# A two-layer diffusion trunk on one core: 16384 experts per layer, gathered per token before, evaluated densely after

## The chip, the cores and the metric

The kernel runs on one core of one Trainium2 chip. The metric is the device time of one execution in microseconds, the median of several runs. All arrays are float32 before and after the change.

## What is computed

The trunk has two layers over 512 latent tokens and 256 context tokens of width 1024. Each layer is a mixer (a projection, four mLSTM heads, eight attention heads, an output projection, a norm) and then the PEER sub-layer, the only part that the change touches. In layer 0 it works on all 768 tokens (six tiles of 128), in layer 1 on the 512 latent ones (four tiles).

```python
q = (ub @ wq).reshape(tb, 8, 2, 128)
s1 = einsum('thd,hnd->thn', q[:, :, 0], sub_keys[:, 0])   # 128 keys per half
s2 = einsum('thd,hnd->thn', q[:, :, 1], sub_keys[:, 1])
t1, i1 = top_k(s1, 16);  t2, i2 = top_k(s2, 16)
top, pos = top_k(t1[..., :, None] + t2[..., None, :], 16)  # of 256 candidates
eidx = the 16 expert numbers i1 * 128 + i2 of each of 8 heads
g = softmax(top)
act = gelu(einsum('td,tkd->tk', ub, up[eidx]))             # 128 experts per token
y = einsum('tk,tkd->td', g * act, down[eidx])
```

`up` and `down` have 16384 rows of 1024 per layer. A token uses 128 of them (8 heads by 16). The kernel keeps both in one array, `updown`, with rows of 2048 numbers (8 KB): up first, then down.

## The kernel before

Five engines run their own programs and meet at barriers (`meet`) between stages. Conditioning rows come first, then for each layer projection, mLSTM and attention, the output projection with the first norm (L676 to L698 on TensorE, which also folds the query weights and the sub-keys into `wk`), and then the expert stage. The norm after the experts closes the layer.

The expert stage goes tile by tile, head by head, slot by slot: 128 slots per tile. A slot is one expert per token. POOL gathers 128 rows of 8 KB for it by an indirect DMA (L976) into one of eight ring buffers. DVE multiplies the up half by the modulated token and sums it (L1312). ACT takes the gelu (L920). DVE builds a diagonal matrix of gelu times gate (L1305, `make_diag`). TensorE multiplies that diagonal by the down half in two matmuls of 512 columns, which add into two PSUM banks (L723, `weigh`). Meanwhile the routing of the head after next is cut into steps that DVE runs between the slots (`route`, L1232): the scores come from TensorE (L715, eight matmuls of 256 columns per head). There are 1280 slots in the two layers. A slot's buffer comes free when its matmuls are done (`L.slot_done`), and only then is its next gather issued.

The order around the change is set by semaphores alone: TensorE's order is the program's, SP issues the loads of each stage in a fixed list, and POOL has nothing to do but the gathers.

Of the kernel before, what the change touches and what calls it, by code (L numbers as in the profile page):

```python
# [12 lines left out]
F32 = mybir.dt.float32  # L13
# [6 lines left out]
P = 128  # L20
D = 1024
KD = D // P
L = 2
# [21 lines left out]
RING = 8  # L45
EXP_AT, NORM_AT = 11, 14
LEAD = 2


C_ID, C_ROT, C_TRI, C_IOTA, C_KEEP, C_MASK, C_COS, C_SIN, C_END = 0, 128, 256, 512, 528, 528, 1552, 2064, 2576  # L50


def shape_constants():
# [11 lines left out]
    c[:, C_IOTA:C_IOTA + TOPK] = np.arange(TOPK)  # L65
# [85 lines left out]
def tile_spans(l):  # L151

    return [(0, 1), (1, 2), (2, NT - 1), (NT - 1, NT)] if l < L - 1 else [(0, NT - NCT - 1), (NT - NCT - 1, NT - NCT)]
# [47 lines left out]
def build(nc, xin, cT, consts, ada_w, ada_b, w_in, wg, bg, convw, ml_norm_w, bias, w_out, ln1, wqT, keysT,  # L203
          updown, ln2, mod_d, negm_d, out):
    with ExitStack() as ctx:
# [12 lines left out]
        iota = CN[:, C_IOTA:C_IOTA + TOPK]  # L218

# [97 lines left out]
        wk_flat = wk.rearrange("p k n -> p (k n)")  # L317
        sc2r, sh2r = r(D), r(D)
        keys_at = r.at
        u = r(D)  # L320
        u_next = r(D)
        uTs = r(KD, P)
        g2r = r(D)
        ln2r = r(2, D)
        junk = r(D)
        prod = junk.bitcast(BF16).rearrange("p (a d) -> p a d", a=2)
        diag = r(2, P)
        zero = r(P)
        idx16 = r(TOPK).bitcast(U32)
        sc = r(2, NKEY)  # L330
        cand2 = sc.rearrange("p a b -> p (a b)")
        tv = r(2, TOPK)
        ti = r(2, TOPK).bitcast(U32)
        cand = r(256)
        oh = cand
        tt = r(TOPK)
        pos = r(TOPK).bitcast(U32)
        hilo = r(2, TOPK).bitcast(U32)
        e1 = r(2, TOPK)
        eidx_all = r((NT + 1) * PH * TOPK).bitcast(U32)  # L340
        gate_all = r((NT + 1) * PH * TOPK)
        gsum = r(PH)
        dots = r(TOPK)
        acts = r(TOPK)
# [3 lines left out]
        ring = r(RING, 2 * D)  # L348
# [16 lines left out]
        sd = r(2)  # L365

# [35 lines left out]
        def _(e):  # L402
# [16 lines left out]
            for l in range(L):  # L419
# [62 lines left out]
                for c in range(2 * PH):  # L482
                    if c >= len(wq_slots):
                        e.wait_ge(sem("L.wk_mm"), 2 * (c - len(wq_slots) + 1))
                    e.dma_start(wq_slots[c % len(wq_slots)], wqT[l, c * P:(c + 1) * P, :]).then_inc(sem(f"L.wq_loaded{c % len(wq_slots)}"), 16)
                    if c == 0:
                        e.dma_start(ln1r[:].rearrange("p a b -> p (a b)"), ln1[l:l + 1, :].to_broadcast([P, 2 * D])).then_inc(sem("L.row1_loaded"), 16)
                    if c == 2:
                        if l < L - 1:
                            mod_row(g1r[:, 1], 1, G1, "L.row1_loaded")  # L490
                        mod_row(sc2r, cnd, SC2, "L.u_rows_loaded")
                        mod_row(sh2r, cnd, SH2, "L.u_rows_loaded")
                meet(e, "sp")

                mod_row(g2r, cnd, G2, "L.row2_loaded")
                e.dma_start(ln2r[:].rearrange("p a b -> p (a b)"), ln2[l:l + 1, :].to_broadcast([P, 2 * D])).then_inc(sem("L.row2_loaded"), 16)
                if l < L - 1:
                    e.wait_ge(sem("L.u_ready"), NCT)
                    mod_row(sc2r, 1, SC2, "L.u_rows_changed")
                    mod_row(sh2r, 1, SH2, "L.u_rows_changed")  # L500
                    e.wait_ge(sem("L.acc_free"), NCT + 1)
                    mod_row(g2r, 1, G2, "L.g_row_changed")
# [11 lines left out]
        def _(e):  # L514
# [17 lines left out]
            for l in range(L):  # L532
# [167 lines left out]
                nt = NT - t0  # L700

                def turn_u(t):

                    e.wait_ge(sem("L.u_ready"), t + 1)
                    for k in range(KD):
                        mm = e.transpose(ps[4 + k // 4][:, (k % 4) * P:(k % 4 + 1) * P], u_next[:, k * P:(k + 1) * P], ident)  # L706
                    mm.then_inc(sem("L.uT_mm"), 1)

                def key_scores(unit, h, lead):

                    if lead < 2 or unit >= 1:
                        e.wait_ge(sem("L.route_read"), unit + 2 - lead)
                    bank = ps[2 + (unit % 2 if lead == 2 else 0)]
                    for k in range(KD):
                        mm = e.matmul(bank[:, 0:2 * NKEY], uTs[:, k, :], wk_flat[:, bass.ds(h * (2 * NKEY) + k * (2 * PH * NKEY), 2 * NKEY)],  # L715
                                      start=(k == 0), stop=(k == KD - 1))
                    mm.then_inc(sem("L.key_mm"), 1)

                def weigh(n, k):

                    e.wait_ge(sem("L.diag_ready"), n + (k + 1))
                    for hf in range(2):
                        mm = e.matmul(ps[hf][:], diag[:, k % 2, :], ring[:, k % RING, D + hf * 512:D + (hf + 1) * 512],  # L723
                                      start=False, stop=False, skip_group_check=True)
                    mm.then_inc(sem("L.slot_done"), 1)

                def tile(t, more):
                    e.wait_ge(sem("L.acc_free"), t + 1)
                    for hf in range(2):
                        e.matmul(ps[hf][:], zero, ln2r[:, 0, 0:512], start=True, stop=False, skip_group_check=True)  # L730
                    if more:
                        turn_u(t + 1)
                    with e.Fori(0, PH - LEAD) as h:
                        key_scores(t * PH + h + LEAD, h + LEAD, 1)
                        for k in range(TOPK):
                            weigh(t * (PH * TOPK) + h * TOPK, k)
                    if more:
                        e.wait_ge(sem("L.uT_ready"), t + 2)
                        e.sem_inc(sem("pe_token"), 1)
                    with e.Fori(0, LEAD) as h:  # L740
                        if more:
                            key_scores(t * PH + h + PH, h, 1)
                        for k in range(TOPK):
                            weigh(t * (PH * TOPK) + h * TOPK + (PH - LEAD) * TOPK, k)
                    for hf in range(2):
                        mm = e.matmul(ps[hf][:], zero, ln2r[:, 0, 0:512], start=False, stop=True, skip_group_check=True)
                    mm.then_inc(sem("L.acc_ready"), 1)

                turn_u(0)
                e.wait_ge(sem("L.uT_ready"), 1)  # L750
                for h in range(LEAD):
                    key_scores(h, h, 2)
                e.wait_ge(sem("L.row2_loaded"), 32)
                e.wait_ge(sem("L.zero_set"), 2)
                for ta, tb in tile_spans(l):
                    if tb - ta > 1:
                        with e.Fori(ta, tb) as t:
                            tile(t, True)
                    else:
                        tile(ta, tb < nt)  # L760
# [6 lines left out]
        def _(e):  # L767
# [4 lines left out]
            for l in range(L):  # L772
# [128 lines left out]
                nt = NT - t0  # L901

                def keep_uT(t):
                    e.wait_ge(sem("L.uT_mm"), t + 1)
                    e.sem_inc(sem("act_token"), 1)
                    e.wait_ge(sem("L.key_mm"), t * PH)
                    e.sem_inc(sem("act_token"), 1)
                    for j in range(2):
                        ins = e.activation(uTs[:, 4 * j:4 * j + 4, :], ps[4 + j][:, :].rearrange("p (k n) -> p k n", k=4), ACT.Copy)
                    ins.then_inc(sem("L.uT_ready"), 1)  # L910

                def gate_exp(un):
                    e.wait_ge(sem("L.route_done"), un + 1)
                    e.sem_inc(sem("act_token"), 1)
                    e.activation(gate_all[:, bass.ds(un * TOPK, TOPK)], gate_all[:, bass.ds(un * TOPK, TOPK)], ACT.Exp).then_inc(sem("L.gexp"), 1)  # L915

                def unit(un, route):
                    for k in range(TOPK):
                        e.wait_ge(sem("L.dot_done"), un * TOPK + (k + 1))
                        e.activation(acts[:, k:k + 1], dots[:, k:k + 1], ACT.Gelu_apprx_tanh).then_inc(sem("L.act_done"), 1)  # L920
                        if k == EXP_AT and route:
                            gate_exp(un + LEAD)

                def tile(t, more):
                    with e.Fori(0, PH - LEAD) as h:
                        unit(t * PH + h, True)
                    if more:
                        keep_uT(t + 1)
                    with e.Fori(0, LEAD) as h:
                        unit(t * PH + h + (PH - LEAD), more)  # L930
                    e.wait_ge(sem("L.var2"), t + 1)
                    e.activation(sd2[:, 0:1], mv2[:, 1:2], ACT.Sqrt, bias=epsc[:, 0:1]).then_inc(sem("L.sd2"), 1)

# [4 lines left out]
                for h in range(LEAD):  # L938
                    gate_exp(h)
# [506 lines left out]
```

## Time and profile before

| | |
|---|---|
| time, 3 runs | 4857.22 us median, 4848.95 to 4857.74 |
| span of the profiled execution, core 0 | 4851.8 us |
| its own time | given by its span: no other time is recorded for it |
| TensorE busy | 4056.9 us, 84% |
| VectorE busy | 3217.5 us, 66% |
| GpSimd busy | 1502.4 us, 31% |
| ScalarE busy | 843.4 us, 17% |
| mean granted TensorE clock | 0.952 |

PE is TensorE's matmuls and PEld its weight loads, which run beside them. DVE is VectorE, ACT ScalarE, POOL GpSimd; SP issues DMAs. L723 is line 723 of the kernel. A row of the groups says how often an instruction ran, its busy time and the mean of one. Instructions of PE are pipelined: the recorded length of one (592 ns) overlaps the next, and the step from one to the next is read from a chain or timeline row with many of them. The granted clock is a share of full speed, 2.4 GHz.

### The profile page before, as it was taken

The page shows a single profiled execution, that of the slowest core. Times are in us where ns is not written, and L with a number is a line of the kernel's source. Part 1 is how long each engine was busy: PE and PEld are TensorE (multiplying, and loading weights), DVE is VectorE, ACT ScalarE, POOL GpSimd, SP SyncE. Part 2 cuts the span into 40 slices and gives each one's busy share as a digit, 9 for nine tenths or more (in the row PEclk, how much of TensorE's full clock was granted, in tenths as well). Part 3 has the DMA queues.
Part 4 walks back from the last instruction along what each step waited for, and adds up shares of the span by engine and source line. Part 5 has one row for each costly group of instructions (what it writes and reads, how often), then busy time and mean ns, then how long its engine had stood idle before and what let it go on. Part 6 is the DMA issues. An engine that isn't in the chain of part 4 may idle for free.

```text
span 4851.8 us, 47489 instructions
## 1 busy us (share of the span) xinstructions
PE 4056.9 (84%) x11304; PEld 1920.3 (40%) x11304; DVE 3217.5 (66%) x8492; ACT 843.4 (17%) x2182; POOL 1502.4 (31%) x1349
## 2 busy tenths in 40 slices
PE   8999899687887887887888879989788788788887
PEld 1354675333333333333333324456433333333332
DVE  0220864787777887787787863065588787778776
ACT  0100341111111111111111111023111111111111
POOL 0000010344443443443444430001144344344443
PEclk9999799999999999999999999989899999999999
DMA  9411112999998998998999982122499899899998
GB/s 325 161 52 50 66 63 77 365 416 404 376 417 364 420 414 341 411 418 337 420 418 385 416 334 72 38 98 83 170 411 419 343 414 413 335 418 416 391 412 355
DMA packets 260491, 1484.23 MB, mean 306 GB/s; under 512 B 23943, under 2 KB 48775, under 8 KB 95767
## 3 DMA queue, kind: packets, MB, share of 16 engines
q0 software_dynamic: 184320, 1342.26, 67.3%
q1 hardware_dynamic: 76060, 140.67, 8.5%
q8 instruction: 48, 0.79, 0.1%
q14 instruction: 63, 0.51, 0.0%
HBM read 1476.40 MB, written 2.24 MB: 305 GB/s over the span
## 4 chain that ended last, share of the span: by engine, by line
PE 51%; DVE 26%; issue 15%; DMA 6%; DVEq 2%; ACT 1%; POOL 0%; SPq 0%; POOLq 0%; ACTq 0%
PE ps L723 22%; PE ps L715 6%; DMA arena<-in_updown,arena 5%; PE ps L565 4%; DVE arena L1312 3%; DVE arena L1305 3%; PE ps L522 3%; PE ps L580 3%; PE ps L683 3%; PE ps L585 2%; DVE arena L1275 1%; PE ps L652 1%; DVE arena L1280 1%; DVE arena L1278 1%; PE ps L608 1%
## 5 line engine op out<-in xcount | busy, mean ns | idle before, releaser
L723 PE MATMUL ps<-arena 128*128 128x512 f32 x5120 | 2433.3, 620 | 537.8 <-DVE arena L1305 534.7
L976 POOL DMA_INDIRECT arena<-in_updown,arena x1280 | 1461.4, 1142 | 2225.6 <-PE ps L723 1717.8
L723 PEld LDWEIGHTS ps<-arena 128*128 128x128 f32 x5120 | 938.2, 194 | 2000.5 <-DVE arena L1305 1157.6
L1312 DVE CUSTOM_DVE_ANT_0 arena<-arena 128x1024 bf16<-128x1024 f32 x1280 | 1563.2, 1221 | 173.5 <-DMA arena<-in_updown,arena 107.5
L920 ACT ACTIVATE arena<-arena 128x1 f32<-128x1 f32 x1280 | 252.2, 202 | 2726.3 <-DVE arena L1312 2688.5
L1305 DVE TENSOR_SCALAR arena<-CN,arena 128x128 f32<-128x128 f32 x1280 | 440.9, 344 | 85.6 <-ACT arena L920 46.7
L963 POOL TENSOR_TENSOR arena<-arena 128x256 f32<-128x256 f32 x64 | 40.7, 667 | 1092.9 <-DMA arena<-in_bias 1092.9
L715 PE MATMUL ps<-arena 128*128 (+1 forms) x1280 | 302.4, 391 | 2.3 <-ACT arena L936 2.3
L1237 DVE MAX8 arena<-ps 128x8 f32<-128x128 f32 x80 | 24.0, 299 | 388.4 <-PE ps L715 388.2
L715 PEld LDWEIGHTS ps<-arena 128*128 128x128 f32 x1280 | 252.7, 198 | 68.5 <-issue 32.5
L565 PE MATMUL ps<-arena 128*128 128x512 f32 (+1 forms) x672 | 233.5, 508 | 0.0
L522 PE MATMUL ps<-arena,sT 128*2 128x512 f32 x384 | 166.6, 596 | 14.3 <-DMA arena<-in_ada_w 14.3
L920 ACT ACT_TABLE_LOAD x136 | 174.5, 1283 | 10.9 <-issue 7.6
L565 PEld LDWEIGHTS ps<-arena 128*128 128x128 f32 x672 | 128.9, 192 | 104.7 <-issue 97.7
L580 PE MATMUL ps<-arena 128*128 128x512 f32 x352 | 151.4, 592 | 0.0
L683 PE MATMUL ps<-arena 128*128 128x512 f32 x320 | 139.1, 593 | 1.0 <-DVEq L382 1.0
L991 DVE SCALAR_TENSOR_TENSOR arena<-ps,arena 2x512 f32<-2x512 f32 x24 | 16.3, 679 | 165.3 <-PE ps L522 165.3
L706 PE MATMUL ps<-CN,arena 128*128 128x128 f32 x80 | 18.9, 415 | 120.6 <-DVE arena L1330 112.6
L915 ACT ACT_TABLE_LOAD x78 | 100.1, 1283 | 35.0 <-DVE arena L1285 31.0
L1312 DVE DVE_READ_ACCUMULATOR2_ANT arena<- 128x1 f32 x1280 | 105.2, 82 | 0.0
L608 PEld LDWEIGHTS ps<-arena 128*128 128x128 f32 x624 | 88.3, 227 | 34.6 <-issue 15.6
L608 PE MATMUL ps<-arena 128*128 128x129 f32 x624 | 95.8, 318 | 7.0 <-DVE arena L1116 5.5
(184 smaller groups left out, 2894.6 us busy)
## 6 DMA issues: line engine op xcount, KB each, us to landing
arena<-in_ada_w SPq DMA_DIRECT2D x24, 2048.0 KB, 7.9
arena<-in_updown,arena POOLq DMA_INDIRECT x1280
arena<-in_wq SPq DMA_DIRECT2D x32, 512.0 KB, 4.3
arena<-in_w_in SPq DMA_DIRECT2D x6, 2048.0 KB, 8.8
arena<-in_w_in SPq DMA_DIRECT2D x24, 512.0 KB, 3.8
arena<-in_bias SPq DMA_DIRECT2D x16, 512.0 KB, 3.6
arena<-in_w_out SPq DMA_DIRECT2D x2, 4096.0 KB, 13.4
arena<-negm_rows SPq DMA_DIRECT2D x16, 384.0 KB, 4.4
```

What stands on the lines that cost most here:

```text
L522: mm = e.matmul(ps[n % 4][0:2, :], sT[:, k, :], adaw[:, n % 3, k, :], start=(k == 0), stop=(k == KD - 1))
L565: mm = e.matmul(bank[:, 0:width], wch[:, c % 3, k, :], uT[:, k, cols], start=(k == 0), stop=(k == KD - 1))
L580: mm = e.matmul(bank[:], uT[:, k, i * P:(i + 1) * P], wtok[:, s, k, :], start=(k == 0), stop=(k == KD - 1))
L608: mm = e.matmul(bank[:, d * (DV + 1):(d + 1) * (DV + 1)], WD2[h % 2][:, d, at(i, j):at(i, j) + P], vml[:, i, h, :], start=(i == src[0]), s ...
L683: mm = e.matmul(ps[2 * (m % 2) + hf][:], mixT[:, k, t * P:(t + 1) * P], wo[:, k, hf * 512:(hf + 1) * 512], start=(k == 0), stop=(k == KD - 1))
L715: mm = e.matmul(bank[:, 0:2 * NKEY], uTs[:, k, :], wk_flat[:, bass.ds(h * (2 * NKEY) + k * (2 * PH * NKEY), 2 * NKEY)], start=(k == 0), st ...
L723: mm = e.matmul(ps[hf][:], diag[:, k % 2, :], ring[:, k % RING, D + hf * 512:D + (hf + 1) * 512], start=False, stop=False, skip_group_chec ...
L915: e.activation(gate_all[:, bass.ds(un * TOPK, TOPK)], gate_all[:, bass.ds(un * TOPK, TOPK)], ACT.Exp).then_inc(sem("L.gexp"), 1)
L920: e.activation(acts[:, k:k + 1], dots[:, k:k + 1], ACT.Gelu_apprx_tanh).then_inc(sem("L.act_done"), 1)
L976: e.indirect_dma_start(ring[:, k % RING, :], None, updown, bass.IndirectOffsetOnAxis(ap=idx16[:, k:k + 1], axis=0)).then_inc(sem(f"rows{k ...
L1305: e.tensor_scalar(diag[:, k % 2, :], ident, acts[:, k:k + 1], gate_all[:, bass.ds(un * UN + k, 1)], ALU.mult, ALU.mult).then_inc(sem("L.di ...
L1312: e.tensor_tensor_reduce(prod[:, k % 2, :], ring[:, k % RING, 0:D], u, 1.0, 0.0, ALU.mult, ALU.add, dots[:, k:k + 1]).then_inc(sem("L.dot_ ...
```

## The change

The slot loop is gone. Every expert is evaluated for every token, in two phases per layer, and the spilled product of phase one is read back in phase two.

Phase one, per group `e` of 128 experts (128 groups): SP loads the up rows (512 KB, one of four buffers); TensorE turns them (U: eight transposes), ACT copies the result; TensorE multiplies it with the turned tokens `pT` (H: eight matmuls of 384 columns for each of two passes in layer 0, of 512 columns for one pass in layer 1); ACT writes the gelu to a staging tile, and POOL stores every second one to DRAM (`peer_h`). Beside it runs the routing: scores for all heads of a tile come from 32 matmuls of 512 columns (S, ahead of all groups), DVE finds the top 16s (`heads`, `lookups`), ACT the exponent (E), TensorE turns expert numbers and gates (R). Then, for groups of eight tokens, DVE builds one-hot rows (`one_hots`), and TensorE multiplies two of them per token into a 128 by 128 gate matrix (G), which ACT copies out and POOL stores 2 MB at a time (`peer_g`).

`PeerJobs` writes TensorE's order of all that from estimated costs: it keeps a clock for TensorE and one for DVE, and puts a G job into the list after the H job at which DVE should have its input; what is left when the groups are over goes at the end.

Phase two, per block of four groups (32 blocks per pass): SP loads 2 MB of down rows, the gelus and the gates; DVE multiplies these two (`weights`), and TensorE multiplies the result with the down rows into two PSUM banks per tile: three tiles per pass in layer 0 (two passes), four in layer 1. `finish` is the norm.

```diff
+UP_RING, HG_RING, DOWN_RING = 4, 3, 3
+JB = 4
+NBLK = NKEY // JB
+def passes(l):
+    return [(0, 3), (3, 6)] if l < L - 1 else [(0, 4)]
+class PeerJobs:
+    US = dict(T=0.5, S=3.5, U=0.45, R=0.4, G=0.45, E=0.0)
+    HEADS4, LOOKUPS, NORM, GROUP, MARGIN = 26.0, 15.0, 2.0, 4.2, 7.0
...
+        for e in range(NKEY + 1):
+            if e < NKEY:
+                self.add("U", e, 0)
+                self.add("U", e, 1)
+            for g in range(self.npass if e >= 1 else 0):
+                self.add("H", e - 1, g)
+                self.place(todo, at, False)
+        self.place(todo, at, True)
...
+            done = max(self.dve, need) + us
+            if what and not rest and done + self.MARGIN > self.now:
+                return
...
+        self.now += self.US[kind] if kind in self.US else KD * self.width * 0.00084
@@ SP
+                e.wait_ge(sem("L.route_done"), pj.nt)
+                for b in range(DOWN_RING):
+                    load_down(b)
+                for s in range(2):
+                    e.wait_ge(sem(f"gates_stored{s}"), g_before[l] + 16 * (pj.nt * (P // TB) // 2))
+                load_hg(0)
+                e.wait_ge(sem("L.peer_mm"), pj.mm_of("U", NKEY - 1, 1))
+                load_hg(1)
...
+                for b in range(HG_RING, np_ * NBLK):
+                    e.wait_ge(sem("L.block_mm"), b - HG_RING + 1)
+                    load_down(b)
+                    load_hg(b)
@@ TensorE
-                    for hf in range(2):
-                        mm = e.matmul(ps[hf][:], diag[:, k % 2, :], ring[:, k % RING, D + hf * 512:D + (hf + 1) * 512],
+                        for k in range(KD):
+                            mm = e.matmul(bank[:], pT[:, k, t * P:(t + 1) * P], wk[:, k, hp * 512:(hp + 1) * 512], start=(k == 0), stop=(k == KD - 1))
...
+                        for k in range(4):
+                            mm = e.transpose(bank[:, k * P:(k + 1) * P], up[:, i % UP_RING, (4 * j + k) * P:(4 * j + k + 1) * P], ident)
...
+                        for k in range(KD):
+                            mm = e.matmul(bank[:, 0:w], upT[:, i % 2, k, :], pT[:, k, c:c + w], start=(k == 0), stop=(k == KD - 1))
...
+                        if j % 2 == 0:
+                            e.wait_ge(sem("L.onehot_ready"), g + 1)
+                        for a in range(4):
+                            o = (4 * (j % 2) + a) * NKEY
+                            mm = e.matmul(bank[:, a * P:(a + 1) * P], ab[:, g % 2, 1, o:o + NKEY], ab[:, g % 2, 0, o:o + NKEY], start=True, stop=True)
...
+                    for j in range(JB):
+                        o = j * w + (q - q0) * P
+                        for hf in range(2):
+                            mm = e.matmul(ps[2 * acc + hf][:], hb[s].rearrange("p a b -> p (a b)")[:, o:o + P], down[:, b % DOWN_RING, j, hf * 512:(hf + 1) * 512],
@@ ScalarE
+                    elif kind == "U":
+                        ins = e.activation(upT[:, i % 2, 4 * j:4 * j + 4, :].rearrange("p a b -> p (a b)"), bank[:], ACT.Copy)
+                    elif kind == "H":
+                        ins = e.activation(hst[:, i // 2 % 2, j, (i % 2) * w:(i % 2 + 1) * w], bank[:, 0:w], ACT.Gelu_apprx_tanh)
@@ GpSimd
-                        e.indirect_dma_start(ring[:, k % RING, :], None, updown,
+                    if kind == "H" and i % 2 == 1:
+                        e.wait_ge(sem("L.peer_evac_a"), pj.evac[n][1])
+                        e.dma_start(h_d[l][j, i // 2], hst[:, i // 2 % 2, j, 0:2 * pj.width])
+                    if kind == "G" and j % 8 == 7:
+                        e.wait_ge(sem("L.peer_evac_a"), pj.evac[n][1])
+                        e.dma_start(g_d[l][tb], gst[:, tb % 2, :])
@@ VectorE
+                def one_hots(i, j):
+                    g = i * (P // GRP) + j
+                    if j == 0:
+                        e.wait_ge(sem("L.peer_evac_a"), pj.evac_of("R", i, 0))
+                    if g >= 2:
+                        e.wait_ge(sem("L.peer_mm"), pj.mm_of("G", (g - 2) // (P // GRP), 2 * ((g - 2) % (P // GRP)) + 1))
+                    e.tensor_tensor(B, keys_b, e2T, ALU.is_equal)
+                    ch.link(e.tensor_tensor(A, keys_b, e1T, ALU.is_equal))
+                    e.tensor_tensor(B, B, gT, ALU.mult).then_inc(sem("L.onehot_ready"), 1)
...
+                    e.tensor_tensor(hv, hv, gv, ALU.mult).then_inc(sem("L.weights_ready"), 1)
```

## Rows read from the trace of the kernel before

**Rows 1.** The page: busy time by engine, and the DMA queue of the gathers.
```profile
PE 4056.9 (84%) x11304; PEld 1920.3 (40%) x11304; DVE 3217.5 (66%) x8492; ACT 843.4 (17%) x2182; POOL 1502.4 (31%) x1349
...
q0 software_dynamic: 184320, 1342.26, 67.3%
```

**Rows 2.** Stretches: busy us of PE, PEld, DVE, ACT, POOL, granted clock, DMA share, GB/s.
```profile
300.00:400.00 100.00, 100.00 (x275) 52.03 (x274) 4.74 (x8) 4.74 (x9) 0.00 (x0) 1.00 0.17 56
500.00:600.00 100.00, 87.57 (x434) 64.49 (x434) 84.45 (x295) 28.72 (x63) 5.81 (x10) 0.81 0.19 72
1000.00:1500.00 500.00, 410.33 (x977) 180.83 (x978) 400.16 (x1090) 85.31 (x243) 218.89 (x192) 0.98 0.98 404
3000.00:3100.00 100.00, 100.00 (x266) 50.35 (x265) 7.67 (x12) 4.35 (x8) 0.00 (x0) 1.00 0.14 45
```

**Rows 3.** The chain that ended last: start us, us, engine, line, records.
```profile
727.93 3.57 PE ps L695 x32
731.50 13.75 PE ps L683 x32
...
979.50 15.76 PE ps L723 x36
995.26 3.47 PE ps L715 x16
1019.59 15.76 PE ps L723 x36
```

**Rows 4.** Groups by line: busy us, mean ns, idle time before and what ended it.
```profile
L723 PE MATMUL ps<-arena 128*128 128x512 f32 x5120 | 2433.3, 620 | 537.8 <-DVE arena L1305 534.7
L976 POOL DMA_INDIRECT arena<-in_updown,arena x1280 | 1461.4, 1142 | 2225.6 <-PE ps L723 1717.8
...
L683 PE MATMUL ps<-arena 128*128 128x512 f32 x320 | 139.1, 593 | 1.0 <-DVEq L382 1.0
...
L898 ACT ACTIVATE arena<-ps 128x512 f32<-128x512 f32 x64 | 33.9, 597 | 4.4 <-PE ps L695 4.4
...
L1278 DVE TENSOR_TENSOR arena<-arena 128x256 f32<-128x256 f32 x160 | 66.9, 418 | 0.3
...
L1222 DVE TENSOR_TENSOR arena<-arena 128x1024 f32<-128x1024 f32 x10 | 12.3, 1226 | 0.3
...
L1335 DVE COPY arena<-arena 128x1024 f32<-128x1024 f32 x10 | 6.9, 694 | 25.6 <-remote 23.2 <-DVE X L1362 1.8 <-DVE arena L1300 0.6
```

**Rows 5.** Timeline of TensorE: transposes (L553, L641) and what follows.
```profile
189.84 8.33 PE L553 MATMUL ps<-CN,X 128*128 128x128 f32 x48 [0.64 <-POOLq L382]
199.09 20.80 PE L560 MATMUL ps<-arena 128*8 128x512 f32 x64 [0.93 <-DVE arena L1060]
...
596.36 0.66 PE L641 MATMUL ps<-CN,arena 128*128 128x128 f32 x4
596.86 1.06 PE L652 MATMUL ps<-arena 128*128 128x128 f32 x8
```

**Rows 6.** Timeline at the ends of the expert stages and the kernel's end.
```profile
833.69 0.33 SPq L479 DMA_DIRECT2D arena<-mod_rows  x1
...
2894.50 1.02 PE L746 MATMUL ps<-arena 128*128 128x512 f32 x2
2911.38 7.79 PE L553 MATMUL ps<-CN,X 128*128 128x128 f32 x48 [15.86 <-POOLq L382]
...
3452.34 0.33 SPq L479 DMA_DIRECT2D arena<-mod_rows  x1
...
4838.56 1.88 PE L746 MATMUL ps<-arena 128*128 128x512 f32 x4
```

**Rows 7.** Timeline of DVE: the first and last step of one head's search.
```profile
845.63 0.30 DVE L1237 MAX8 arena<-ps 128x8 f32<-128x128 f32 x1 [8.90 <-PE ps L715]
...
851.34 0.17 DVE L1270 TENSOR_SCALAR arena<-arena 128x16 uint32<-128x16 uint32 x1
```

**Rows 8.** DMA issues: count, KB each, median us from issue to landing.
```profile
arena<-in_ada_w SPq DMA_DIRECT2D x24, 2048.0 KB, 7.9
...
arena<-in_w_in SPq DMA_DIRECT2D x24, 512.0 KB, 3.8
arena<-in_bias SPq DMA_DIRECT2D x16, 512.0 KB, 3.6
arena<-in_w_out SPq DMA_DIRECT2D x2, 4096.0 KB, 13.4
```

**Rows 9.** Timeline of SP: three issues of 1024 pieces each.
```profile
2913.90 8.69 SPq L437 DMA_DIRECT2D arena<-in_w_in  x3
```

More of the change, by code:

```diff
@@ L316, in build @@
         wk = r(KD, 2 * PH * NKEY)
[L317 to L344, printed above, removed]
+        keys_at = wk_top = r.at
+        r = Region()
+        hst = r(2, 2, 1024)
+        gst = r(2, NKEY * TB)
+        ab = r(2, 2, GRP * NKEY)
+        assert r.at <= wk_top
+        r = Region(wk_top)
+        pT = r(KD, T)
+        scores_at = r.at
+        scores = r(NT * PH, 2 * NKEY)
+        up_at = r.at
+        up = r(UP_RING, D)
+        temps_at = r.at
+        ti = r(2 * PH, TOPK).bitcast(U32)
+        tv = r(4, TOPK)
+        sc = r(4, NKEY)
+        cand = r(2, 256)
+        cand2 = sc.rearrange("p (a b) n -> p a (b n)", a=2)
+        tt = r(PH, TOPK)
+        pos = r(PH * TOPK).bitcast(U32)
+        hilo = r(2, PH * TOPK).bitcast(U32)
+        gsum = r(2, PH)
+        e12 = r(2, 2, PH * TOPK)
+        gl = r(2, PH, TOPK)
+        rT = r(2, 3, P)
+        r.at = max(r.at, temps_at + 4096)
         lns2 = r(2, 6)
@@ L347, in build @@
         sd2 = r(2)
-        ring = r(RING, 2 * D)
+        upT = r(2, KD, P)
+        down = Region(scores_at)(DOWN_RING, JB, D)
+        assert DOWN_RING * JB * D <= up_at - scores_at
+        hg_at = [temps_at, up_at, wk_top]
+        hb = [Region(a)(JB, 512) for a in hg_at]
+        gb = [Region(a + 2048)(2048) for a in hg_at]
+        r = Region()
+        ybuf = r(2, D)
+        g2r = r(2, D)
+        ln2r = r(2, D)
         keys = Region(keys_at)(2 * PH, NKEY)
@@ new lines, in _ @@
+                e.wait_ge(sem("L.route_done"), pj.nt)
[6 more added lines that the diff above has]
+                load_hg(1)
+                for s in range(2):
+                    for g in range(np_):
+                        e.wait_ge(sem(f"acts_stored{s}{g}"), h_before[l] + 16 * (NKEY // 4))
@@ L698, in _ @@
                 meet(e, "pe")
[L700 to L717, printed above, removed]
@@ L749, in _ @@
[L749 to L758, printed above, removed]
-                    else:
-                        tile(ta, tb < nt)
+                pj = peer[l]
@@ L899, in _ @@
                 meet(e, "act")
[L901 to L931, printed above, removed]
-                    e.activation(sd2[:, 0:1], mv2[:, 1:2], ACT.Sqrt, bias=epsc[:, 0:1]).then_inc(sem("L.sd2"), 1)
-                e.wait_ge(sem("L.uT_mm"), 1)
@@ L935, in _ @@
-                for j in range(2):
-                    ins = e.activation(uTs[:, 4 * j:4 * j + 4, :], ps[4 + j][:, :].rearrange("p (k n) -> p k n", k=4), ACT.Copy)
-                ins.then_inc(sem("L.uT_ready"), 1)
-                for h in range(LEAD):
-                    gate_exp(h)
-                for ta, tb in tile_spans(l):
-                    if tb - ta > 1:
-                        with e.Fori(ta, tb) as t:
-                            tile(t, True)
-                    else:
-                        tile(ta, tb < nt)
+                pj = peer[l]
@@ L946, in _ @@
+                for q in range(pj.nt):
+                    e.wait_ge(sem("L.var2"), q + 1)
+                    e.activation(sd2[:, 0:1], mv2[:, 1:2], ACT.Sqrt, bias=epsc[:, 0:1]).then_inc(sem("L.sd2"), 1)
                 if l < L - 1:
@@ new lines, in _ @@
+                pj = peer[l]
+                w = pj.width
+                for n, (kind, i, j) in enumerate(pj.jobs):
+                    if kind == "T" and pj.evac[n][0] == "v":
+                        cnd, wd, tc = (1, SEQ, slice(CTX, T)) if j == "x" else (0, CTX, slice(0, CTX))
+                        e.wait_ge(sem("L.peer_mm"), pj.mm[n])
+                        e.tensor_scalar(pT[:, i, tc], ps[pj.bank[n]][:, 0:wd], modcol[:, l, SC2 * KD + i, cnd:cnd + 1], modcol[:, l, SH2 * KD + i, cnd:cnd + 1],
+                                        ALU.mult, ALU.add).then_inc(sem("L.peer_evac_v"), 1)
@@ new lines, in _ @@
+                for i in range(pj.nt):
+                    heads(i, 0)
+                    heads(i, 1)
+                    if i >= 1:
+                        gate_norm(i - 1)
+                    heads(i, 2)
+                    heads(i, 3)
+                    lookups(i)
+                    for j in range(P // GRP if i >= 1 else 0):
+                        one_hots(i - 1, j)
+                        if i == pj.nt - 1 and j == P // GRP // 2:
+                            gate_norm(i)
+                for j in range(P // GRP):
+                    one_hots(pj.nt - 1, j)
@@ new lines, in _ @@
+                ready = 0
+                for g, (q0, q1) in enumerate(passes(l)):
+                    while ready < (g + 1) * NBLK:
+                        weights(ready)
+                        ready += 1
+                    if g == 0:
+                        e.wait_ge(sem("L.row2_loaded"), 48 if l < L - 1 else 32)
+                    for q in range(q0, q1):
+                        e.wait_ge(sem("L.acc_ready"), q + 1)
+                        finish(q)
+                        if ready < pj.npass * NBLK:
+                            weights(ready)
+                            ready += 1
@@ L1396 @@
+                if l < L - 1:
+                    meet(e, "dve")
+                    reset(e, "dve", "L.", ch)
 def kernel(**inputs):
```

491 lines of the change are left out of this document (286 added, 205 removed).

## The prediction

> **What bounds the kernel now.** I read the page's busy line first. TensorE is busy 84% and VectorE 66%, which names no bound, because the stages differ [rows 1]. The stretches tell them apart. In the projection (300 to 400 us, 3000 to 3100 us) TensorE is busy all the time at the full clock and DMA is at 0.14 to 0.17. In the expert stage (1000 to 1500 us) DMA is at 0.98 and 404 GB/s, while TensorE has 410 of 500 us and VectorE 400 [rows 2]. So the expert stage runs at the speed of its gathers: 1342 MB go through their queue [rows 1], 1.05 MB per slot. The chain shows the pace. The same two pieces come back after 1019.59 - 979.50 = 40.1 us for 16 slots [rows 3], so 2.5 us per slot, 419 GB/s. The seams give the length of the two expert stages: 833.7 to 2895.5 us (2061.8) and 3452.3 to 4840.4 us (1388.1) [rows 6]. Together they are 3450 of 4851.8 us. All else, 1402 us, is kept: 833.7 ahead, 15.9 from the last matmul of layer 0 to the next projection, 540.9 of layer 1's mixer, 11.4 at the end [rows 6]. SP's two fewer row loads ahead of the stage lie beside the output projection and change nothing there.
>
> **What a matmul costs.** This price decides the case. L683 has 160 float32 matmuls of 512 columns (ten tiles, two halves, eight steps) and 320 records [rows 4]: two records per matmul. 32 records, 16 matmuls, take 13.75 us of the chain [rows 3]: 0.4297 us per record, **0.859 us per matmul**. Key scores of 256 columns: 16 records in 3.47 us [rows 3], 0.217 per record. On the line between, 384 columns give 0.323 per record and 0.647 us per matmul. Products of 128 columns: 32 records (16 matmuls) in 3.57 us [rows 3], 0.223 us each. Weight loads lie under all of these. The order list of the change reckons with 0.43 us for 512 columns (3.5 us for eight): the length of one record, half of what I read.
>
> A transpose is one record: four take 0.50 us at full clock (596.36 to 596.86), 0.125 us each; 48 at the stage's start take 8.33 us, 0.174 each [rows 5]. I take 0.125, since the new ones run in a dense stream; the other end adds 100 us over 2048 of them, and the lower end, one record of a 128-column product (0.112), takes off 27. The row shows a transpose 1.8 times as fast as an ordinary product of its size. The Trainium skill, "TensorE: Matmul & The Clock Gate", Terms, calls the transpose mode four times faster for float32. By that rule one would take about 0.056 us and the sum would be some 140 us lower; the row disagrees, and I stay with it.
>
> **The change part by part, TensorE's column.** Layer 0:
> - T, the first 48 transposes and their copies: 9.3 us, from 189.84 to 199.09 [rows 5].
> - S: 24 x 8 = 192 matmuls x 0.859 = 165.
> - U: 1024 transposes x 0.125 = 128; R 18 more, 2.
> - H: 128 groups x 2 passes x 8 = 2048 x 0.647 = 1324.
> - G beside the groups: 152 of the 192 jobs x 4 x 0.223 = 136.
> - G at the end (below): 71.
> - the turn from phase one to two (below): 22.
> - down products: 2 passes x 128 x 3 tiles x 2 = 1536 x 0.859 = 1320.
> Sum 3177 us.
>
> Layer 1: T 5 (32 transposes), S 128 x 0.859 = 110, U and R 130, H 1024 x 0.859 = 880, G 104 jobs x 0.892 = 93, end of G 41, turn 22, down 1024 x 0.859 = 880. Sum 2161 us.
>
> **The end of G.** Walking through the costs in PeerJobs, its list still holds 40 G jobs (20 token groups) after the last H in layer 0 and 24 jobs (12 groups) in layer 1. They have no H to hide behind. A group costs DVE three operations of 1024 elements, 1.226 us each [rows 4], with gaps 3.75 us, and TensorE only 1.8. The one-hot buffers are two, so DVE is never more than two groups ahead. The end then runs at DVE's pace: 1.8 + 18 x 3.75 + 1.8 = 71 us, and 1.8 + 10 x 3.75 + 1.8 = 41. If the comparisons ran like a copy, 0.694 us [rows 4], the two would be 46 us shorter; double the price would add about 105. I take 1.226, since L1278, a product with a broadcast operand, fits the same line (418 ns for 256) [rows 4].
>
> **The turn.** Phase two's first gate load waits for the last 2 MB gate store, though it needs other tiles. After the last G: the copy 0.6 (L898), POOL's issue about 1.1 (L976) [rows 4], the store 7.9 like other 2 MB transfers [rows 8], then SP issues the gelu load and 1536 or 2048 pieces of gates at 8.69 / 3 = 2.9 us per 1024 [rows 9], 5 to 6.5 with the gelus. Landing behind the issue about 2 to 3, under the 3.8 of 512 KB [rows 8], DVE's product 1.8 or 2.3 on the 1278-1222 line [rows 4]. That is 19 to 22, and with a few matmuls at a fallen clock 22. Bounds: 12 if transfers overlap more, 40 if the store through POOL's queue takes twice as long.
>
> **What I cost at nothing.** DVE's routing per tile: eight searches x 5.9 us (845.63 to 851.51) [rows 7], six lookups of 2048 elements at 2.3, 16 groups at 3.75, together 121 us; 726 and 484 us per layer lie beside 1836 and 1260 us of phase one. Since TensorE needs twice what the list supposes, G jobs come later than planned, after their input, and DVE's ring of two fills without holding TensorE. ACT has two copies and two gelus per group, each about 0.6 [rows 4], beside over 11 us. The up loads are 512 KB per 8 to 11 us of TensorE and land in about 4 [rows 8]. In phase two a block moves 3.7 MB (layer 1: 4.2), 9 to 10.4 us at the 404 GB/s of [rows 2], with two blocks of 20.6 (27.5) us ahead. At the change of pass the last two blocks go tile by tile, so the norm of the first tile (8 us) is over while TensorE still has two tiles. Only the last norm stands alone, as before.
>
> **Sum.** 1402 + 3177 + 2161 = 6740 us of span, against 4851.8. The median of the runs is 5.4 above the profiled span; I predict **6745 us**, 39% slower. Of the stage's 5338 us, 4908 are ordinary float32 products at a price seen in rows; the uncertain terms are small. Own range: 6650 (transposes at 0.112, quick one-hots, short turns: -27 - 46 - 20) to 6890 (transposes at 0.174, longer turns, half of the dearer one-hots).
>
> **The rivals.**
> 1. *A matmul costs one record.* The order list's 0.43 us per 512 columns holds for the new products: 4908 halves, and the time is about **4290 us, faster**. It would win from 0.53 us per 512 columns on (4908 x (1 - 0.53 / 0.859) = 1880). For it speaks only the list. Against it: 320 records for 160 matmuls, and the same types and shapes after. 3%. Beside it, the Trainium skill, "TensorE: Matmul & The Clock Gate", Back-to-back issue gap, gives N / 2.4 + 2.5 ns, 216 ns at 512 columns; taken for a whole float32 matmul it would make 3060 us. The trace has it four times dearer, so this gets no more of the chance.
> 2. *The clock falls in the long dense stage.* At 0.98, the gathers' stage's value [rows 2], it adds 105 us (6850, inside the range). At 0.81, the mLSTM stretch's, it adds 1200: about 7950. Rows 2 show 1.00 wherever TensorE is dense, and the lower values where it pauses. 4% for a fall that leaves the range.
> 3. *The one-hots hold TensorE all along*, because the list's clocks are wrong: at worst DVE's 1210 us stand in a row, 7950 us. It decides once DVE needs more than TensorE between two G jobs, 4 us against 10 or more. 4%.
> 4. *The loads of phase two aren't hidden* (thin pieces, one issue queue): 64 x 10.9 + 32 x 12.7 = 1100 us, 7850. Against it: issuing takes 5 to 8 us of 20 to 27. 3%.
> The forecast keeps 86%.
>
> **How the numbers follow.** The likeliest case gives 6745. Rivals 3 and 4 would come in part if at all, and take in the same upper end, so the range is 6650 to 6890 and leaves out about 2 in 10 with the errors of the terms. A change of 0.2%, 10 us, is about the least that a measurement of this kernel can tell. Faster is rival 1 alone: 0.03. Within 0.2%: 0.005. Slower: 0.965.
>
> **What would show it.** TensorE dense at clock 1.00 in both expert stages, DMA at a third or less of its share; H records 0.32 us apart in layer 0 and 0.43 in layer 1; phase two at 20.6 and 27.5 us per block; about 70 and 40 us at phase one's end in which TensorE waits for DVE, then some 20 us of DMA wait. Records of 512 columns that are one per matmul would overturn it.

## Result and profile after

6693.77 us, median of 4 runs (6692.89 to 6697.97), against 4853.09 (4 runs) of the kernel before: ratio 1.379, 95% interval 1.377 to 1.381. The profiled span is 6692.7 us, clock 0.983.

The page of the kernel after (busy time; DMA queues: packets, MB, share; shares of the chain):

```profile
PE 6486.2 (97%) x21366; PEld 3479.4 (52%) x21366; DVE 1901.8 (28%) x4042; ACT 990.7 (15%) x1890; POOL 165.2 (2%) x301
...
q1 hardware_dynamic: 354236, 640.94, 29.8%
q0 software_dynamic: 25216, 167.79, 6.1%
...
PE 93%; DVE 4%; DMA 1%; issue 1%; ACT 1%; DVEq 0%; SPq 0%; POOL 0%; ACTq 0%; POOLq 0%
```

The gathers' 1342 MB [rows 1] are gone, TensorE has risen from 84% to 97%, and 93% of the chain is its own. Its groups by line (L889 is H, L910 the down product, L900 G, L883 the transposes of the up rows):

```profile
L889 PE MATMUL ps<-arena 128*128 128x384 f32 x4096 | 1349.0, 486 | 0.0
...
L889 PE MATMUL ps<-arena 128*128 128x512 f32 x2048 | 899.9, 592 | 0.0
L910 PE MATMUL ps<-arena 128*128 128x512 f32 x5120 | 2202.9, 593 | 36.0 <-DVE arena L1499 35.7
...
L900 PE MATMUL ps<-arena 128*128 128x128 f32 x2560 | 313.6, 276 | 43.0 <-DVE arena L1475 43.0
...
L883 PE MATMUL ps<-CN,arena 128*128 128x128 f32 x2048 | 265.6, 273 | 0.6 <-ACT arena L1104 0.6
```

2048 H matmuls of layer 0 left 4096 records: two per matmul, as L683 before [rows 4]; H never waited. The down products waited 36 us in all, two turns. The chain gives the steps; the down products stand there in whole pieces, one per pass (two in layer 0, one in layer 1):

```profile
1008.25 10.32 PE ps L889 x32
1019.44 10.32 PE ps L889 x32
...
2661.43 662.48 PE ps L910 x1536
3324.19 659.45 PE ps L910 x1536
...
5800.59 881.06 PE ps L910 x2048
```

An H record of 384 columns takes 10.32 / 32 = 0.3225 us. From one group's H to the next are 11.19 us, so the eight transposes between take 0.87, 0.109 each. 3983.6 - 2661.4 = 1322 us for 1536 matmuls is 0.861 each. The stretches of layer 0 after (as in [rows 2]; phase one, its end, the turn, phase two):

```profile
1010.00:2560.00 1550.00, 1550.00 (x6259) 1009.13 (x6258) 524.12 (x1191) 357.73 (x678) 77.82 (x144) 1.00 0.30 103
2579.00:2645.00 66.00, 38.40 (x305) 35.30 (x304) 63.01 (x54) 22.74 (x39) 2.14 (x4) 1.00 0.32 134
2645.00:2661.00 16.00, 0.00 (x0) 0.00 (x0) 1.43 (x1) 1.83 (x2) 0.53 (x1) 0.56 0.79 284
2661.00:3983.00 1322.00, 1321.27 (x3071) 584.60 (x3072) 148.11 (x114) 1.47 (x5) 0.00 (x0) 1.00 0.52 173
```

TensorE is dense at 1.00 in both phases. Between them stand 66 us in which DVE is busy for 63 and TensorE for 38, and 16 us in which TensorE does nothing. TensorE's timeline at that end, and after the turn:

```profile
2577.14 3.85 PE L900 MATMUL ps<-arena 128*128 128x128 f32 x32
2582.89 2.02 PE L900 MATMUL ps<-arena 128*128 128x128 f32 x16 [1.90 <-DVE arena L1475]
2586.41 2.02 PE L900 MATMUL ps<-arena 128*128 128x128 f32 x16 [1.51 <-DVE arena L1475]
...
2642.89 2.02 PE L900 MATMUL ps<-arena 128*128 128x128 f32 x16 [1.51 <-DVE arena L1475]
2661.43 4.61 PE L910 MATMUL ps<-arena 128*128 128x512 f32 x5 [16.51 <-DVE arena L1499]
```

Two token groups come in a row, then one every 3.53 us, each released by the third one-hot operation. The chain through the turn (start us, us):

```profile
2645.84 6.52 DMA peer_g<-arena
...
2652.85 6.63 DMA arena<-peer_g
...
2659.57 1.77 DVE arena L1499
...
2661.43 3.75 PE ps L910 x4
```

The last gate store lands, then the first gate load, then DVE multiplies.

### The profile page after: what moved, and what is told of

Its sections match the earlier page's. It is cut to its first block, busy times and chain, and to the rows that moved or that the text cites. A ratio compares the mean times of both kernels' runs of the same rounds, so it can differ in the third digit from the quotient of the medians.

```text
span 6692.7 us, 51731 instructions
## 1 busy us (share of the span) xinstructions
PE 6486.2 (97%) x21366; PEld 3479.4 (52%) x21366; DVE 1901.8 (28%) x4042; ACT 990.7 (15%) x1890; POOL 165.2 (2%) x301
## 4 chain that ended last, share of the span: by engine, by line
PE 93%; DVE 4%; DMA 1%; issue 1%; ACT 1%; DVEq 0%; SPq 0%; POOL 0%; ACTq 0%; POOLq 0%
PE ps L910 33%; PE ps L889 33%; PE ps L878 4%; PE ps L900 4%; PE ps L883 3%; PE ps L725 3%; PE ps L682 2%; PE ps L740 2%; PE ps L843 2%; PE ps L745 1%; PE ps L812 1%; PE ps L768 1%; PE ps L720 1%; PE ps L801 1%; PE ps L790 1%
## 5 line engine op out<-in xcount | busy, mean ns | idle before, releaser
L889 PE MATMUL ps<-arena 128*128 128x384 f32 (+1 forms) x6144 | 2248.9, 521 | 0.0
L910 PE MATMUL ps<-arena 128*128 128x512 f32 x5120 | 2202.9, 593 | 36.0 <-DVE arena L1499 35.7
L910 PEld LDWEIGHTS ps<-arena 128*128 128x128 f32 x5120 | 974.4, 190 | 1263.2 <-issue 1263.2
L889 PEld LDWEIGHTS ps<-arena 128*128 128x128 f32 x6144 | 1144.3, 190 | 926.9 <-issue 429.0
L1473 DVE TENSOR_TENSOR arena<-CN,arena 128x1024 f32<-128x1024 f32 x160 | 195.9, 1224 | 1725.2 <-PE ps L900 1605.6
L1106 ACT ACTIVATE arena<-ps 128x384 f32<-128x384 f32 (+1 forms) x384 | 201.9, 526 | 1924.8 <-PE ps L889 1924.8
L900 PEld LDWEIGHTS ps<-arena 128*128 128x128 f32 x2560 | 308.5, 192 | 93.3 <-ACT arena L1112 43.4
L900 PE MATMUL ps<-arena 128*128 128x128 f32 x2560 | 313.6, 276 | 43.0 <-DVE arena L1475 43.0
L1104 ACT ACTIVATE arena<-ps 128x512 f32<-128x512 f32 x512 | 277.3, 598 | 0.5 <-PE ps L883 0.5
L878 PE MATMUL ps<-arena 128*128 128x512 f32 x640 | 275.1, 592 | 2.1 <-DVE arena L1402 1.2
L883 PEld LDWEIGHTS ps<-CN,arena 128*128 128x128 f32 x2048 | 236.7, 141 | 67.1 <-issue 54.3
L883 PE MATMUL ps<-CN,arena 128*128 128x128 f32 x2048 | 265.6, 273 | 0.6 <-ACT arena L1104 0.6
L1112 ACT ACTIVATE arena<-ps 128x512 f32<-128x512 f32 x320 | 191.0, 597 | 148.1 <-PE ps L900 148.1
L878 PEld LDWEIGHTS ps<-arena 128*128 128x128 f32 x640 | 121.4, 190 | 154.7 <-issue 152.1
L1475 DVE TENSOR_TENSOR arena<-arena 128x1024 f32<-128x1024 f32 x160 | 196.0, 1225 | 5.5
L1474 DVE TENSOR_TENSOR arena<-CN,arena 128x1024 f32<-128x1024 f32 x160 | 195.0, 1219 | 0.0
L725 PEld LDWEIGHTS ps<-arena 128*128 128x128 f32 x672 | 128.8, 192 | 104.3 <-issue 97.3
```

Source lines behind the costliest of these rows:

```text
L725: mm = e.matmul(bank[:, 0:width], wch[:, c % 3, k, :], uT[:, k, cols], start=(k == 0), stop=(k == KD - 1))
L878: mm = e.matmul(bank[:], pT[:, k, t * P:(t + 1) * P], wk[:, k, hp * 512:(hp + 1) * 512], start=(k == 0), stop=(k == KD - 1))
L883: mm = e.transpose(bank[:, k * P:(k + 1) * P], up[:, i % UP_RING, (4 * j + k) * P:(4 * j + k + 1) * P], ident)
L889: mm = e.matmul(bank[:, 0:w], upT[:, i % 2, k, :], pT[:, k, c:c + w], start=(k == 0), stop=(k == KD - 1))
L900: mm = e.matmul(bank[:, a * P:(a + 1) * P], ab[:, g % 2, 1, o:o + NKEY], ab[:, g % 2, 0, o:o + NKEY], start=True, stop=True)
L910: mm = e.matmul(ps[2 * acc + hf][:], hb[s].rearrange("p a b -> p (a b)")[:, o:o + P], down[:, b % DOWN_RING, j, hf * 512:(hf + 1) * 512], ...
```

## Experiments on the changed kernel

**1. The order list with measured costs.** Only TensorE's order changes.

```diff
-    US = dict(T=0.5, S=3.5, U=0.45, R=0.4, G=0.45, E=0.0)
+    US = dict(T=0.5, S=6.88, U=0.44, R=0.4, G=0.89, E=0.0)
...
-        self.now += self.US[kind] if kind in self.US else KD * self.width * 0.00084
+        self.now += self.US[kind] if kind in self.US else KD * self.width * 0.00168
```

> The changed kernel; in PeerJobs TensorE's costs are set to what the traces show (S 6.88, G 0.89, H 0.00168 us per column and step instead of 3.5, 0.45 and 0.00084). Only TensorE's order changes: the last G job of layer 0 then comes after group 76 of 128, that of layer 1 after group 84. Theory: the two ends at DVE's pace (67.4 and 39.2 us) shrink to TensorE's own share of these jobs (35.6 and 21.4), and the turns (16.7 and 19.4 us) to about 1 us, since the gates are stored long before: 6693 - 32 - 18 - 34 = 6610 us. Rival: G jobs placed earlier make TensorE wait for the one-hots there, in small pieces: 6650 to 6700.

Measured: 6611.54 us (6609.36 to 6612.66), 82 under the changed kernel, ratio to before 1.362 (1.359 to 1.366); its span is 6610.8. Its chain at the end of phase one:

```profile
2594.74 0.87 PE ps L883 x8
2595.61 20.66 PE ps L889 x64
2616.27 0.02 issue
2616.29 0.50 ACT arena L1106
2616.79 0.14 issue
2616.92 8.39 PE ps L910 x19
```

The end and the turn are gone: the last H is followed by the down products after 0.7 us. The theory said 6610 us; the rival, waits for the one-hots in small pieces at 6650 us or more, falls. So the two ends and turns were what the traces said, and the list's halved costs made them.

**2. H in bf16.** One cast of the tokens, and ACT writes the turned up rows in bf16; the H product reads both. The gates are spilled in bf16 too. The list has the costs of run 1, with H's set to a bf16 product's and two of VectorE's costs lowered (26 to 21 us for the search of four heads, 4.2 to 3.7 for a group of one-hots).

```diff
-        upT = r(2, KD, P)
+        upT = r(KD * P).bitcast(BF16).rearrange("p (r k n) -> p r k n", r=2, k=KD)
...
-                            mm = e.matmul(bank[:, 0:w], upT[:, i % 2, k, :], pT[:, k, c:c + w], start=(k == 0), stop=(k == KD - 1))
+                            mm = e.matmul(bank[:, 0:w], upT[:, i % 2, k, :], pTb[:, k, c:c + w], start=(k == 0), stop=(k == KD - 1))
```

> The changed kernel with the measured costs in its list, and the H products (tokens by up rows) with both operands rounded to bf16; for room the gates are spilled in bf16 too; all other products are float32. Theory: the time of the dense stage is TensorE's records, and a bf16 product has one record at half the step of a float32 record instead of two: 2048 x (0.645 - 0.163) + 1024 x (0.859 - 0.216) = 987 + 658 = 1645 us off TensorE. Phase one then comes near VectorE's routing (112 us per tile, 672 and 448 us, against TensorE's 781 and 557), with an end at VectorE's pace again: about 5000 to 5080 us. Rival A: a bf16 product costs the same time per column as a float32 one: 6610 us. Rival B: phase one is held by loads and stores, not by TensorE: over 6000 us.

Measured: 5203.13 us, ratio to before 1.072 (1.069 to 1.076). Group rows, a piece of the chain, and two stretches, the second at the end of layer 0's phase one:

```profile
L892 PE MATMUL ps<-arena 128*128 128x384 bf16 x2048 | 364.1, 327 | 0.0
...
L1480 DVE TENSOR_TENSOR arena<-CN,arena 128x1024 f32<-128x1024 f32 x160 | 195.3, 1221 | 267.1 <-PE ps L903 267.1
```
```profile
1024.67 2.60 PE ps L892 x16
```
```profile
1010.00:1400.00 390.00, 383.85 (x2755) 291.23 (x2754) 264.18 (x638) 241.05 (x458) 53.56 (x99) 0.99 0.73 239
1640.00:1760.00 120.00, 57.80 (x425) 53.75 (x426) 117.82 (x129) 31.74 (x54) 3.19 (x6) 0.85 0.27 106
```

Now 2048 matmuls leave 2048 records. The chain has 16 of them in 2.60 us, 0.1625 each, against 0.645 for the float32 matmul of the same size: 3.97 times. The Trainium skill, "FP8 and Floating Point Precision", TensorE Precision Notes, calls true float32 four passes through the array; this run agrees. Rivals A and B fall. The time missed the expectation by 120 to 200 us. From the first key score to the first down product of layer 0 are 947 us instead of about 840. Why is read from the trace and was not tested by a run: VectorE waited 267 us, over both layers, for TensorE's gate jobs (second row), with its ring of two full. In the first stretch it is busy 264 of 390 us while TensorE is dense, and in the second it has to catch up, busy 118 of 120 us with TensorE at 58.

**3. All expert products in bf16.** Run 2, and ACT rounds the down rows; gelus and gates are spilled in bf16, and a down load waits for the rounding of the block before it in its buffer instead of for that block's products.

```diff
+                def cast(b):
...
+                    for j in range(JB):
+                        ins = e.activation(down16[:, s, j, :], down[:, s, j, :], ACT.Copy)
+                    ins.then_inc(sem("L.down_cast"), 1)
...
-                        mm = e.matmul(ps[2 * acc + hf][:], hb[s].rearrange("p a b -> p (a b)")[:, o:o + P], down[:, b % DOWN_RING, j, hf * 512:(hf + 1) * 512],
+                        mm = e.matmul(ps[2 * acc + hf][:], hb[s][:, o:o + P], down16[:, b % DOWN_RING, j, hf * 512:(hf + 1) * 512],
```

> As the run with H in bf16, and the down products in bf16 too: ACT rounds the down rows, gelus and gates are spilled in bf16. Key scores, gate products and all else stay float32. Theory (one bf16 record for two float32 records): TensorE's 2203 us of down products become 553, less than the loads: per block 2.1 MB of down rows and 0.8 MB (layer 1: 1.05) of gelus and gates, 7.1 and 7.7 us at 408 GB/s, up to 8.7 and 9.5 at the rate that the thinner pieces allowed so far. The phase turns from TensorE's to DMA's. With the phase ones of the H run (947 and 631 us with their turns): 1402 + 12 + 1578 + 64 x 7.1 to 8.7 + 32 x 7.7 to 9.5 = 3690 to 3850 us, under both kernels. Rival: ACT's rounding or the thin pieces of gates (256 bytes now) hold the blocks at 12 us or more: over 4100 us.

Measured: 3821.13 us (3816.14 to 3821.57), ratio to before 0.787 (0.785 to 0.788): **faster than both kernels**, with the rounding of these operands as its price. It lies in the expected range of 3690 to 3850 us, near its upper end, and the rival (over 4100 us) falls. Layer 0's phase two:

```profile
1760.00:2318.00 558.00, 387.00 (x1569) 163.39 (x1600) 114.45 (x133) 256.48 (x272) 1.06 (x2) 0.90 0.99 327
```

DMA is at 0.99 and 327 GB/s, TensorE at 387 of 558 us with pauses and a granted clock of 0.90. A block takes 558 / 64 = 8.7 us. After what runs 4 to 8 below show of such shares, the share alone is no proof that the loads are the bound. The chain says the same, though: from 1800 to 2300 us 87% of it are loads of down rows. No run with fewer bytes tested it.

## Experiments on the kernel before: what bounded it

The prediction reads the expert stage of before as bound by its gathers. That carried no term of the sum, but it is the first thing a reader takes from it, so it was tested. In all five kernels parts of the work are left out or replaced.

**4. Half of each gather.**

```diff
-                        e.indirect_dma_start(ring[:, k % RING, :], None, updown,
+                        e.indirect_dma_start(ring[:, k % RING, 0:D], None, updown.rearrange("r (h d) -> (r h) d", h=2),
```

> The kernel before, with half of each gather: 4 KB instead of 8 KB per expert (other rows than the chosen ones, and both matmuls of a slot read the same half, so its values are not the model's). Theory: the expert stage of before runs at the speed of its gathers (1.05 MB per 2.5 us slot at 0.98 of the DMA engines), so halving the bytes frees it until the next bound, TensorE and VectorE at 410 and 400 of 500 us, 2.0 us per slot: 1280 slots x 0.45 us less, about 4280 us, at least below 4450. Rival A: the pace is TensorE's (84% busy) with its waits: no change, 4850. Rival B: the pace is set by the number of rows gathered, not their bytes: no change either, but DMA share stays near 0.98.

4779.93 us, ratio 0.985 (0.982 to 0.988): the expectation of 4280 fails. So does rival B, which wanted a DMA share near 0.98: it is 0.62 (first fence below). Rival A, no change, is off by 69 us.

**5. One of the two products per slot.**

```diff
-                    for hf in range(2):
+                    for hf in range(1):
                         mm = e.matmul(ps[hf][:], diag[:, k % 2, :], ...
```

> The kernel before, with one of the two matmuls of 512 columns per slot (the other half of each output row is left out). TensorE loses 1280 x 0.859 = 1100 us of work. Theory (gathers set the pace): within 1% of 4853 us, 4810 to 4870. Rival (TensorE sets the pace): the slot falls towards VectorE's 2.0 us, about 4300 us.

4822.08 us, ratio 0.994 (0.991 to 0.996), inside the expected 4810 to 4870. Its stretch (second fence below) shows the gathers at 0.98 and a clock fallen to 0.71 with TensorE's pauses.

**6. Both edits.**

> The kernel before with both edits of the two earlier runs: gathers of 4 KB per expert and one matmul of 512 columns per slot (values not the model's). Alone they took off 1.5% and 0.65%. Theory: two bounds of nearly the same height stood in the expert stage: the gathers (2.5 us per slot at DMA share 0.98), and a loop per head of 40 us in which DVE searches and dots (about 20 us), then TensorE works off its backlog of 16 slots and the next key scores (15.8 + 3.5 us) while DVE waits 8.9 us for those scores. Either alone hides the other. Taking both away, the backlog halves (minus 7.9 us of 40.1 per head, if TensorE's clock holds): 80 heads x 5 to 7.9 us = 400 to 630 us, 4150 to 4400 us. Rival: the pace is VectorE's or POOL's alone: still over 4700 us.

4614.36 us, ratio 0.950 (0.948 to 0.952). It is 243 us off, more than the two alone (69 and 27 us) and less than the expected 400 to 630. The backlog was read wrongly: 15.8 us are 36 records [rows 3], at four records per slot 9 slots and not 16. And its half is not saved, since VectorE then holds the pace. The granted clock is 0.73 over the stretch (third fence below), but where the backlog was it is 1.00, and TensorE waits there for each diagonal (two rows of its timeline, and the stretch):

```profile
1015.48 1.12 PE L723 MATMUL ps<-arena 128*128 128x512 f32 x2 [0.28 <-DVE arena L1305]
1016.88 1.12 PE L723 MATMUL ps<-arena 128*128 128x512 f32 x2 [0.28 <-DVE arena L1305]
```
```profile
1015.00:1022.00 7.00, 4.71 (x9) 1.19 (x8) 6.16 (x16) 3.48 (x7) 5.64 (x5) 1.00 0.85 262
```

These two slots begin 1.40 us apart, which is VectorE's dot and diagonal, where two float32 matmuls took TensorE 1.72. The clock falls to 0.50 in the search (1002 to 1010 us), where TensorE waits for VectorE anyway.

**7 and 8. The key scores from 2 of 8 steps, with half gathers and with full ones.**

```diff
-                    for k in range(KD):
+                    for k in range(2):
                         mm = e.matmul(bank[:, 0:2 * NKEY], uTs[:, k, :], ...
```

> The kernel before with gathers of 4 KB and the key scores of each head from 2 of their 8 steps (values not the model's); both matmuls per slot stay. Theory of the loop: the scores stand between TensorE's backlog and DVE's next search, so 6 x 0.434 = 2.6 us go from each of 80 heads: 4780 - 208 = 4570 us. Rival (VectorE, POOL or slot latency sets the pace, the scores are beside it): 4780 us as with half rows alone.

> The kernel before with the key scores of each head from 2 of their 8 steps (values not the model's); gathers and both matmuls per slot in full. With half rows the same edit took 204 us off. Theory: with full rows the gathers are the second bound and hide it: 4800 to 4850 us, at most 1% less. Rival: the gathers never bound, the loop of searches and backlog does alone: 4857 - 208 = 4650 us.

Measured 4576.27 us (ratio 0.942, 0.940 to 0.944) with half gathers and 4794.19 us (0.987, 0.986 to 0.989) with full ones. The first is what the loop gives (4570), the second is 6 us under the expected 4800 to 4850 and far from its rival's 4650. The stretches of 4, 5, 6, 7 and 8, one kernel each:

```profile
1000.00:1500.00 500.00, 413.19 (x981) 182.61 (x980) 399.87 (x1089) 85.21 (x243) 230.68 (x193) 0.97 0.62 202
```
```profile
1000.00:1500.00 500.00, 361.46 (x596) 126.32 (x594) 402.56 (x1089) 85.97 (x243) 201.75 (x194) 0.71 0.98 407
```
```profile
1000.00:1500.00 500.00, 366.03 (x622) 128.62 (x622) 421.06 (x1138) 91.19 (x257) 231.63 (x205) 0.73 0.68 213
```
```profile
1000.00:1500.00 500.00, 407.90 (x885) 168.09 (x884) 421.02 (x1125) 92.05 (x256) 248.04 (x201) 0.94 0.67 213
```
```profile
1000.00:1500.00 500.00, 394.25 (x844) 152.74 (x844) 406.78 (x1101) 86.67 (x245) 204.98 (x195) 0.97 0.99 410
```

With half gathers DMA is at 0.62 and the pace hardly changes. The round of a head shows it better than the time: 16 slots, from the first search operation of one head (L1237) to that of the next, read from VectorE's timeline of each run (medians within the tiles).

| run | gathers | TensorE's work | round, us |
|---|---|---|---|
| before | 8 KB | full | 40.1 |
| 4 | 4 KB | full | 40.1 |
| 5 | 8 KB | one product | 38.0 to 42.8, median 39.8 |
| 6 | 4 KB | one product | 38.0 |
| 7 | 4 KB | short scores | 37.5 |
| 8 | 8 KB | short scores | 39.8 |

Halving the gathers alone leaves the round where it was. Of the 74 us by which run 4's span is shorter, about 24 come after the last search of each layer and 25 in longer rounds and at changes of tile; no run tests what makes them. The chains of 4, 7 and 8, one fence each:

```profile
976.38 15.76 PE ps L723 x36
1016.44 15.75 PE ps L723 x36
```

```profile
998.41 15.76 PE ps L723 x36
1014.16 0.88 PE ps L715 x4
1035.93 15.76 PE ps L723 x36
```
```profile
983.02 3.70 PE ps L723 x8
...
1011.25 9.86 DMA arena<-in_updown,arena
1022.79 3.70 PE ps L723 x8
```

In run 7 the round is 1035.93 - 998.41 = 37.5 us instead of the 40.1 of run 4 and of before [rows 3]: just the 2.6 us of the dropped scores, and 4780 - 4576 = 204 us is 80 heads times 2.55. So there is a loop. DVE searches and dots for some 20 us, TensorE then works off 15.8 us of products and the next scores, and DVE waits for these. In the waits of before and of 7 (engine, line waited for, us, times, longest):

```profile
DVE arena L1237 <- PE ps L715: 388.2, 76, 8.9
```
```profile
DVE arena L1237 <- PE ps L715: 184.5, 76, 5.4
```

In run 4 that wait is 383.9 us, so full or half gathers make no difference to it, and the short scores take 199 of run 7's 204 us out of it.

The short scores with full gathers bring only 64 us. DMA stands at 0.99 and 410 GB/s, the round at 39.8 us, and 9.9 us of gathers have come into its chain (last fence). Both bounds are real: the loop at 40.1 us per head and the gathers at 39.8, within 1% of each other. The loop set the round of the kernel before, and the gathers stood right behind it.

## Why the prediction was right

6745 us was forecast, 6693.8 measured, 0.8% less. By its steps:

- **A float32 matmul costs 0.859 us at 512 columns and 0.647 at 384** (4908 of 5338 us). Right: 0.861 and 0.645 in the trace. H, S and the down products of layer 0 came to 1321, 165 and 1322 us against 1324, 165 and 1320. Run 2 shows the cause: at 384 columns one bf16 record at half the step each takes the place of two.
- **Transposes at 0.125 us.** The largest miss, 0.109 in a dense stream: 2078 x 0.016 = 33 us. The end ruled in at 0.112 was nearer than the row chosen, which came from four transposes between other products. The ordinary product beside it takes 0.223, so the ratio is 2. The Trainium skill's factor of 4 ("TensorE: Matmul & The Clock Gate", Terms) is not seen here either; by it the sum would have been 93 us too low instead of 47 too high.
- **The ends of G at DVE's pace.** Right in place, cause and size: 67.4 and 39.1 us against 71 and 41. The group took 3.53 us, not 3.75, because two of DVE's three steps are shorter than its operations: L1474 begins 1.14 us after L1473, and the next L1473 1.14 after L1475, each with 1.22 of recorded work; only L1475, which waits for L1474, comes 1.25 after it. Run 1 removes the ends.
- **The turns, 22 each.** 16.7 and 19.4 us. Right in kind: store, load, product, each behind the other. The store took 6.5 us where 7.9 was taken, and issuing the first gelu and gate loads under 1 us where it was 5 to 6.5; the load landed in 6.6. Run 1 takes the turns away as well.
- **Routing, loads, stores, gelu at nothing.** Right: TensorE was never idle in 1550 us of phase one, and phase two ran at 1322 of 1320 us, 20.7 us per block. One sign on the list failed: DMA was to stay at a third or less, and it is at 0.30 in phase one but 0.52 in phase two. The slack was smaller than thought and still enough.
- **1402 us kept.** Ahead 834.3 us (833.7 forecast), between the layers 15.6 (15.9), layer 1's mixer with its first transposes 546.9 (545.9), the end 11.1 (11.4). The first transposes of layer 0 took 6.6 instead of 9.3.

The misses add up to -33 - 5 - 8 - 3 = -49, and the span differs by 6740 - 6693 = 47 us. The other 4 us are the step from span to median, 5.4 in the forecast and 1.1 here.

**What was wrong** is the reading of the kernel before, "the expert stage runs at the speed of its gathers". A DMA share of 0.98 was taken for the bound, although TensorE and DVE at 0.82 and 0.80 fed each other in a loop without slack, and the 40.1 us of a head were this loop's (run 4). The chain's shares on the page of before, passed over, had pointed to it, with 6% for DMA over the whole kernel:

```profile
PE 51%; DVE 26%; issue 15%; DMA 6%; DVEq 2%; ACT 1%; POOL 0%; SPq 0%; POOLq 0%; ACTq 0%
```

Both bounds were there: the busy share told of one alone, and the chain's 6% made little of gathers that stood 1% behind. It did no harm here, since the change replaced gathers and loop alike.

**The rivals.** The one-record price (rival 1) falls: 4096 records for 2048 matmuls. The clock (2) stayed at 1.00. The one-hots (3) held TensorE at the ends alone. The loads (4) were hidden, at a DMA share of 0.52.

## What to carry to other kernels

Count records per matmul and divide a dense chain piece by their number before pricing a dense rewrite: here one such price was 92% of the new stage. A rewrite that evaluates all 16384 experts where 128 are used paid here only with both expert products in bf16 (3821 us), not with H alone in bf16 (5203) and not in float32 (6694). An order list written from estimated costs should be checked against the first trace: its factor of two cost 82 us. And a resource that is busy 0.98 of the time is not known to be the bound until its work has been halved: here that left the round of a head at 40.1 us.

## What the runs showed that was not expected

- Halving the bytes of a gather (8 KB to 4 KB per row) lowered DMA's share from 0.98 to 0.62 and its rate from 404 to 202 GB/s, so the thinner rows keep the engines busy longer per byte: at the same time per byte the share would have been 0.49.
- Taking work off TensorE can leave it nearly as busy: with one product per slot it has 596 records instead of 977 in 500 us, 39% fewer, and 361 instead of 410 us of busy time, 12% less, while the granted clock falls from 0.98 to 0.71.
- Operations of 1024 elements on VectorE (L1473, L1474) began 1.14 us apart at 1.22 us each where the second did not wait for the first.
